# Rounding every buffer of a one-core encoder kernel up to whole 128-byte lines

## What is computed

```python
h = rmsnorm(x, norm_g)
proj = h @ w_in                                  # 1024 -> 3584
q, k, v, g_attn, u, g_four = jnp.split(proj, ...)
q, k = rmsnorm(q, q_g), rmsnorm(k, k_g)          # 12 heads of 64
for window, dil in ((128, 1), (512, 4), (2048, 16)):
    o, l = dilated_window_attention(q, k, v, rel_bias, window, dil)
    ...
attn = jnp.einsum('pbsh,pbshd->bshd', softmax(lses), outs) * silu(g_attn)
mixed = jnp.fft.fftn(u, axes=(1, 3), norm="ortho").real
four = jnp.einsum('bsgc,gce->bsge', mixed, w_four) * silu(g_four)
y = x + concat([attn, four]) @ w_out             # 1024 -> 1024
```

## The kernel before

| operand of TensorE | before | after |
|---|---|---|
| `ident`, `rows` | 0 | 0 |
| `shared`, `w_hi`, `w_lo`, `u_t`, turned queries and keys, `w_out` | 64 | 0 |
| `h`, `h_hi`, `h_lo`, `mix0` (also third slot of `p`) | 96 | 0 |
| sorted queries, `p0`, `p1`, `p_t` | 32 | 0 |
| `m_hi`, `m_lo`, `mix1` | 0 | 0 |
| slots of `v` | 0, 64, 0 | 0, 36, 72 |
| first key of a tile: dilation 1 | 48, 80, 112, 16 | 112, 16, 48, 80 |
| first key of a tile: dilation 4, dilation 16 | 0, 64 | 64, 0 |

## Time and profile before

### The profile page before, as it was taken

The page is one execution under the profiler, slowest core; times in us unless marked ns, Lnnn a source line. Parts: engine busy times, 40 slices in busy tenths (PEclk is TensorE's granted clock), DMA queues, the critical chain, the costliest instruction groups (busy, mean ns, idle before and its releaser), DMA issues. The chain is left out here.

```text
span 4245.0 us, 83865 instructions
## 1 busy us (share of the span) xinstructions
PE 4158.6 (98%) x28408; PEld 3655.8 (86%) x28408; DVE 2591.9 (61%) x7700; ACT 1705.8 (40%) x4279; POOL 837.4 (20%) x1619
## 2 busy tenths in 40 slices
PE   8999999999999999999899999999999999899999
PEld 7888888887887888888799999999999899688887
DVE  6555555556443444444677776777767677777776
ACT  4223222232111111111466666666666666433332
POOL 0000000000111111002244444444444444100000
PEclk9999999999999999999899999999999999899999
DMA  4333333337555333333346445464454544666665
GB/s 166 123 127 126 117 117 117 127 129 202 183 187 163 120 119 119 113 110 117 104 104 136 107 111 124 103 138 106 112 126 101 134 102 115 210 242 248 241 239 183
DMA packets 562981, 601.63 MB, mean 142 GB/s; under 512 B 200007, under 2 KB 438983, under 8 KB 562420
## 3 DMA queue, kind: packets, MB, share of 16 engines
q1 hardware_dynamic: 479316, 499.64, 38.1%
q0 software_dynamic: 83360, 98.05, 8.5%
HBM read 358.53 MB, written 249.08 MB: 143 GB/s over the span
## 5 line engine op out<-in xcount | busy, mean ns | idle before, releaser
L1407 PE MATMUL att_ps_o<-att_v,att_p_t 128*128 128x104 f32 x6528 | 800.4, 275 | 21.6 <-DMA att_v<-scratch_v 17.4
L1407 PEld LDWEIGHTS att_ps_o<-att_v,att_p_t 128*128 128x128 f32 x6528 | 768.3, 193 | 30.1 <-DMA att_v<-scratch_v 20.0
L1327 POOL DMA_DIRECT2D scratch_o<-att_o x864 | 503.5, 587 | 861.7 <-DVE att_o L1539 815.3
L1469 ACT ACTIVATE att_p<-att_s_b,att_o 128x256 f32<-128x256 f32 (+1 forms) x1152 | 503.5, 488 | 314.5 <-DVE att_o L1532 301.2
L820 PE MATMUL p_ps<-p_w_hi,p_h_hi 128*128 128x512 f32 (+1 forms) x1536 | 572.8, 373 | 0.0
L344 PE MATMUL p_ps<-p_w_hi,p_h_hi 128*128 128x512 f32 (+1 forms) x1536 | 567.7, 370 | 4.3 <-DVE p_w_lo L513 4.3
L820 PE MATMUL p_ps<-p_w_hi,p_h_lo 128*128 128x512 f32 (+1 forms) x1536 | 564.1, 367 | 0.0
L344 PE MATMUL p_ps<-p_w_hi,p_h_lo 128*128 128x512 f32 (+1 forms) x1536 | 563.9, 367 | 0.0
L820 PE MATMUL p_ps<-p_w_lo,p_h_hi 128*128 128x512 f32 (+1 forms) x1536 | 563.8, 367 | 0.0
L344 PE MATMUL p_ps<-p_w_lo,p_h_hi 128*128 128x512 f32 (+1 forms) x1536 | 563.4, 367 | 0.0
L1532 DVE CUSTOM_DVE_ANT_0 att_s_b<-att_ps_s,shared 128x256 f32<-128x256 f32 (+1 forms) x1104 | 388.6, 396 | 47.9 <-PE att_ps_s L1379 44.8
(11 more groups left out here) (187 smaller groups left out, 6967.4 us busy)
## 6 DMA issues: line engine op xcount, KB each, us to landing
att_v<-scratch_v SPq DMA_DIRECT2D x1056, 65.0 KB
scratch_o<-att_o POOLq DMA_DIRECT2D x864, 66.0 KB, 2.7
out_o<-scratch_o SPq DMA_DIRECT2D x144, 396.0 KB, 5.3
p_x<-x SPq DMA_DIRECT2D x48, 512.0 KB, 4.7
scratch_ht<-p_h_hi SPq DMA_DIRECT2D x48, 512.0 KB, 4.9
scratch_ht<-p_h_lo SPq DMA_DIRECT2D x48, 512.0 KB, 5.6
p_h_hi<-scratch_ht SPq DMA_DIRECT2D x48, 512.0 KB, 3.7
p_h_lo<-scratch_ht SPq DMA_DIRECT2D x48, 512.0 KB, 4.6
```

Of the source, the lines that this page charges most:

```text
L1327: pool.dma_start(to, o[u % O][:, t, :]).then_inc(stored[u % O], 16)
L1407: ins = pe.matmul(ps_o[:, col:col + WIDE], p_t[u % 2][0:n, t, e, j, :], v[u % V][0:n, unit.chunk(at, part), e * VW:e * VW + WIDE], start=( ...
L1469: act.activation(p[u % PS][:, t, e, 0:at.w], s_b[u % 2][:, t, e, 0:at.w], ACT.Exp, bias=o[u % O][:, t, PAIR_V + e:PAIR_V + e + 1], scale=- ...
```

## The change

`Core.sb` adds, behind each buffer whose size (rounded up to 32 bytes, 8 words) isn't a multiple of 128 bytes (32 words), a second buffer `<name>_rest` that fills the line. 22 such buffers come into being; no instruction uses them. The three slots of `v` become slices of one buffer, and so do the seven of `o`, so that each needs one filler at most; a slot of `v` then begins 2340 bytes behind the one before it, a slot of `o` 1056 bytes. Every engine's instructions, their order and their waits are the same as before, word for word but for the line numbers, which are 6 higher behind the edit.

```diff
--- before.py
+++ after.py
@@ -56,6 +56,7 @@
 KPAD = 64
 VPAD = 256
 N2 = 64
+LINE, GRAIN = 32, 8
 COS = HD + 2
 
 
@@ -135,7 +136,12 @@
         self.nc, self.io, self.keep = nc, io, ExitStack()
 
     def sb(self, stack, name, shape, dt=F32):
-        return stack.enter_context(self.nc.sbuf_tensor(name, shape, dt))
+
+        buffer = stack.enter_context(self.nc.sbuf_tensor(name, shape, dt))
+        rest = -(-(-math.prod(shape[1:]) // GRAIN) * GRAIN) % LINE
+        if rest:
+            stack.enter_context(self.nc.sbuf_tensor(name + "_rest", [shape[0], rest], dt))
+        return buffer
 
     def ps(self, stack, name):
         return stack.enter_context(self.nc.psum_tensor(name, [P, BANK], F32))
@@ -1229,8 +1235,8 @@
         sb = lambda n, shape, dt=F32: core.sb(st, "att_" + n, shape, dt)
         gain = sb("gain", [P, 1])
         bias = [core.shared[:, 2 * i * BIAS:2 * (i + 1) * BIAS].rearrange("p (e c) -> p e c", e=2) for i in range(2)]
-        v = [sb(f"v{i}", [P, 3, PAIR_V + VW]) for i in range(V)]
-        o = [sb(f"o{i}", [P, 2, PAIR_O]) for i in range(O)]
+        all_v, all_o = sb("v", [P, V, 3, PAIR_V + VW]), sb("o", [P, O, 2, PAIR_O])
+        v, o = [all_v[:, i] for i in range(V)], [all_o[:, i] for i in range(O)]
         s_b = [sb(f"s_b{i}", [P, 2, 2, 2 * P]) for i in range(2)]
         q_sorted = [{n: sb(f"{n}{i}", [P, 2, P], F32R) for n in ("q_hi", "q_lo")} for i in range(Q)]
         zeros = sb("zeros", [P, KPAD])
```

## The result

The changed kernel takes 4227.13 us (median of five runs, 4222.02 to 4231.4), beside 4247.2 us for the kernel before, measured with it (five runs, 4241.35 to 4250.07): a ratio of 0.9949, 95% interval 0.9938 to 0.9961. It is 20 us faster.

The account below looks back on a forecast made before the run. TensorE's matmul pace was taken to bound the kernel. All terms summed to 0, so the forecast was the unchanged median, 4243 us (4242.9), with a range of 4228 to 4252 us and 0.80 on no change.

Parts of the forecast that it names:

- What bounds the kernel: Whole kernel: TensorE, busy 98% of the span, sets the end by its matmul pace and its waits.
- Stationary operands, 512 columns: Projections: stationary operands moving from place 96 to 0 (modulo 128) change nothing, since paces were 0.2331 and 0.2329 us; 0.
- Moving operands of 512 and 256 columns: Weights at place 64 in all projections: bounded between 0 and 208 us faster, middle 13 us, taken as 0.
- Scores, transposes, weighting, the other engines: Attention matmuls, transposes and non-TensorE engines: new places change no pace; 0, with 2 us as dilation 4's slow end.
- loads of v: Packed slots begin 4 and 8 bytes past a multiple of 32, nothing new in kind; 0, waits staying near 17 us.
- One line fewer: Rival: streams starting at 0 touch 16 lines instead of 17, saving 13 us, 4230 us; chance 0.08.
- The whole excess: Rival: misplacement causes all streaming time above one column per cycle, so 208 us go, 4035 us; chance 0.04.
- late loads: Rival: writes of `v` at odd offsets take longer, doubling TensorE's 17.4 us of waits, 4260 us; chance 0.08.
- It doesn't do what it says: Rival: `v` and the keys of dilations 1 and 4 still don't begin at 0; costs nothing, inside the forecast.

Follow-up runs that it names:

- map1: Kernel without the layer: chains of 24 matmuls at 16 by 16 operand places; distance (stationary less moving address, modulo 256) 0 took 226.7 ns, 32 took 233.4.
- before_all64: Kernel before with 64 unused bytes ahead of all later buffers, moving weights at multiples of 128, distances of the three products unchanged: 4249.37 us, ratio 0.9996.
- map2: Kernel without the layer: chains with distances in 4-byte steps, fewer columns, or one column repeated; one repeated moving column took 0.2157 us a step.
- before_vo: Kernel before with only the slots of `v` and `o` packed as slices of one buffer each, no fillers: 4246.86 us, ratio 0.9998.
- before_both: Kernel before with gaps of 224 bytes ahead of `h_hi` and 192 ahead of `m_hi`, so distance 0 in all three products: 4200.11 us, ratio 0.9878.
- map3: Kernel without the layer: 96 matmuls at one distance behind three different lead chains; 256 columns at distance 128 took 0.1200 or 0.1186 us.
- after_h384: Changed kernel with 384 unused bytes before the first `h_hi`, bringing both projections to distance 0: 4193.71 us, ratio 0.9869.
- after_h128: Changed kernel with 128 unused bytes before the first `h_hi`, the same modulo 256 as 384 bytes: 4195.63 us, ratio 0.9875.

## Why the prediction was wrong, step by step

**What bounds the kernel** held: TensorE's pace sets the end, and the question was the 0.0198 us above one column per cycle.

**The step that failed is the pricing of each operand by its own place**, in "Stationary operands, 512 columns" and "Moving operands of 512 and 256 columns", both put at 0. The first took "nothing for stationary operands that move from 96 to 0" from two equal paces, 0.2331 and 0.2329. The rows were read rightly; the inference varied one operand's place, called that the variable, and dropped the other's. Those pairs are at distances 32 and 64, which map1 prices at 233.4 and 233.5 ns. Two equal points do not show a flat line where six of the eight distances in map1's table lie within 1 ns of each other. In the output projection only the moving operand changed its place, so there it was the moving term that failed: it measured -13.6 us (2304 matmuls x (233.3 - 226.7) ns = 15 us by the steps). Both projections together, where both places changed, measured -3.3 us: 512 columns gained a little and 256 columns lost. The trace of before had two pairs of places for 512 columns and could not show the third; an honest bound would have been "unknown for any other pair", not 0.

**The rows that decided the moving term** were of 256 columns. One of them, dilation 16, was at distance 0 already and with 0.1189 us no faster than the projection's 256 columns at distance 32, 0.1178. map1 shows why that says nothing of 512 columns: at distance 0 256 columns have 120.0 ns, nearly the most of their row, and 512 columns 226.7, the least of theirs. What held is that the moving place alone counts for nothing: before_all64 moves it to the start of a line, keeps the distance, and the time stays. As a bound the term was wrong in kind too, since all of the excess was put on the moving side. Of the whole excess, 208 us, distance 0 gives back 6.6 of 20 ns a matmul; the remaining 13.4 are there at every distance tried, and nearly all of them go only where the moving address stands still. There the Trainium skill's formula for an isolated warm matmul, on its page "TensorE: Matmul & The Clock Gate" (Back-to-back issue gap), agrees: 215.8 ns for 512 columns, 215.7 in map2. For a moving operand that walks the traces are 11 to 22 ns above it.

**Scores, transposes, weighting, the other engines** held, as the rows after show; the lo x hi scores of the first sequence, half of them of dilation 1, which these rows leave out, last 286 ns in the mean before and after. One count was wrong and cost nothing: after the change `v` begins at eighteen different places, not fourteen. The **loads of v** held: 15.9 us, and before_vo shows that packing alone changes nothing.

**The rivals.** "One line fewer" gave 4230 us, nearly the time, by a mechanism that isn't there: it spread 13 us over all streams, and two thirds of the gain sit in a fifth of them; before_all64 takes the line away and gains nothing. Even its sign, steps of 0.232 in the projections, came, for they are at distance 128 now. A right sum is not a shown cause. "The whole excess" and "late loads" did not come. "It doesn't do what it says" was nearer than I priced it: the change does put operands at the same place of a line of 128 bytes, and that isn't the condition. Of the three products that it brought there, one landed at distance 0 and two at 128; that any landed at 0 is luck.

**The range** missed by 1 us. Its low end rested on the one-line case, and its middle on 4242.9 us, the median of three runs; the kernel before has 4247 to 4250 in the later measurements, so with nothing added the middle was 4 us low already, and the same range around 4247 would have missed by 5.

## What to carry to other kernels

Where chains of 512-column matmuls with new weights of 128 columns each time run above one column per cycle, look at the address of the weights less that of the moving operand, modulo 256, and try 0 by a gap of a few words: here two gaps were worth 1.2% of the whole kernel (before_both). Before a trace is used to say that a place doesn't matter, write down for each pair of matmuls all quantities in which they differ, the differences of addresses too, and ask how many values of each were seen.

## What the runs showed of the hardware

- A chain of rounded-float32 matmuls of 512 columns and 128 weight columns, at 2.4 GHz, takes 226.7 ns a step at distance 0, 228.9 at 192 and 232.2 to 234.3 at the other multiples of 32, repeating every 256 bytes (map1); plain float32 with 104 columns takes 111.6 to 111.7 ns at every distance.
- With 256 columns distance 0 has 120.0 ns, nearly the most in map1's row, and the other multiples of 32 have 113.3 to 120.2 in map1 to map3, not always the same from one map to the next. With 448 columns 96 and 192 are faster than 0 (200.0 beside 202.7 ns), with 320 all four tried are equal (146.7 ns). So distance 0 is good for 512 columns, not a rule.
- Which of several paces a chain of 256 columns takes can depend on the chain ahead of it, at distances 96 and 128 (map3).
- In the attention the granted clock falls to 1.2 GHz for stretches that differ between executions; 27.2 us of it go with a stage of 1596.4 us (after_h384), 54.5 us with one of 1603.8 (after_h128).
